# Rounded head means and a second half ordered by input tile, in the retention stage of a two-block transformer kernel

## The reference, cut to what matters

```python
def head_group_norm(y):
    yf = y.astype(jnp.float32)
    mu = jnp.mean(yf, axis=-1, keepdims=True)
    var = jnp.mean(jnp.square(yf - mu), axis=-1, keepdims=True)
    return (yf - mu) * lax.rsqrt(var + GN_EPS)
...
    ret = head_group_norm(ret).reshape(ret.shape[0], seq, RET_WIDTH)
    ret = (jax.nn.silu(rg.astype(jnp.float32)) * ret).astype(x.dtype)
    mixed = jnp.concatenate([fox.astype(x.dtype), ret], axis=-1)
    h = h + mixed @ w_out[i]
```

## Time and profile before

| | us |
|---|---|
| median of 3 runs | 2307.85 (2307.75 to 2309.3) |
| the profiled execution | 2308.38 |
| its span in the profile | 2306.6 |
| TensorE busy (matmuls) | 2280.4, 99% of the span |
| GpSimd, VectorE, ScalarE busy | 1182.7, 1102.6, 854.6 |

### The profile page before, as it was taken

One profiled execution on the slowest core, in us unless ns is written; L12 is line 12 of the kernel. 1 busy time (PEld: TensorE's weight loads), 2 busy tenths in 40 slices (PEclk: granted clock), 3 DMA queues, 4 the chain that ended last, 5 costly groups with the idle time before them and its releaser, 6 DMA issues.

```text
span 2306.6 us, 34053 instructions
## 1 busy us (share of the span) xinstructions
PE 2280.4 (99%) x11030; PEld 1814.7 (79%) x11030; DVE 1102.6 (48%) x1876; ACT 854.6 (37%) x1295; POOL 1182.7 (51%) x1554
## 2 busy tenths in 40 slices
PE   8999999999999999999999999999999999999997
PEld 6777877688888888877688888887877788888886
DVE  5468857534312314446755253354256755242444
ACT  4354454554322224323443222245233343232254
POOL 5446653345545445543356556566534256555563
PEclk9999999999999999999999999999999999999999
DMA  4221112133223232333222323223332223323222
GB/s 169 87 92 51 56 65 87 56 100 118 95 97 109 82 100 91 112 128 101 92 86 93 107 89 109 83 82 110 102 131 93 78 101 100 101 91 109 82 92 83
DMA packets 67367, 219.64 MB, mean 95 GB/s; under 512 B 8368, under 2 KB 8752, under 8 KB 67264
## 3 DMA queue, kind: packets, MB, share of 16 engines
q1 hardware_dynamic: 58400, 197.66, 25.7%
q10 hardware_dynamic: 8864, 20.62, 2.8%
HBM read 211.92 MB, written 2.13 MB: 93 GB/s over the span
## 4 chain that ended last, share of the span: by engine, by line
issue 42%; POOL 39%; PE 14%; DVE 2%; POOLq 1%; ACT 1%; DMA 1%; DVEq 0%; ACTq 0%; SPq 0%
POOL w_lo L2069 38%; PE acc L335 4%; PE acc L337 4%; PE acc L336 4%; POOLq L2116 1%; PE sc L524 1%; PE po_pt L651 0%; PE po_pt L481 0%; PE sc L651 0%; PE po_pt L460 0%; POOLq L2065 0%; DMA x<-in_x 0%; DMA raw<-in_w_ple_gate 0%; POOLq L2077 0%; DVE x_queries L1627 0%
## 5 line engine op out<-in xcount | busy, mean ns | idle before, releaser
L2069 POOL TENSOR_TENSOR w_lo<-raw,w_hi 128x256 fp32r<-128x256 f32 x1486 | 1134.5, 797 | 1056.5 <-ACT w_hi L854 1052.9
L335 PE MATMUL acc<-act_hi,w_hi 128*128 128x512 f32 x1696 | 673.0, 397 | 9.1 <-DVE act_lo L1387 8.1
L337 PE MATMUL acc<-act_hi,w_lo 128*128 128x512 f32 x1696 | 661.9, 390 | 0.0
L336 PE MATMUL acc<-act_lo,w_hi 128*128 128x512 f32 x1696 | 661.2, 390 | 0.0
L854 ACT CAST w_hi<-raw 128x1024 fp32r<-128x1024 f32 (+1 forms) x388 | 390.6, 1017 | 407.3 <-PE acc L337 224.5
L335 PE MATMUL acc<-y_hi,w_hi 128*128 128x512 f32 x1068 | 421.1, 394 | 0.0
L337 PE MATMUL acc<-y_hi,w_lo 128*128 128x512 f32 x1068 | 416.0, 390 | 0.0
L336 PE MATMUL acc<-y_lo,w_hi 128*128 128x512 f32 x1068 | 415.7, 389 | 0.0
L335 PEld LDWEIGHTS acc<-act_hi,w_hi 128*128 128x128 f32 x1696 | 319.1, 188 | 80.1 <-issue 9.8
L337 PEld LDWEIGHTS acc<-act_hi,w_lo 128*128 128x128 f32 x1696 | 318.9, 188 | 67.6
L336 PEld LDWEIGHTS acc<-act_lo,w_hi 128*128 128x128 f32 x1696 | 319.4, 188 | 65.7 <-issue 1.9
(11 more groups left out here) (316 smaller groups left out, 2097.9 us busy)
## 6 DMA issues: line engine op xcount, KB each, us to landing
raw<-in_w_ffn_wide SPq DMA_DIRECT2D x120, 512.0 KB, 3.3
raw<-in_w_in SPq DMA_DIRECT2D x102, 512.0 KB, 3.3
raw<-in_w_rest SPq DMA_DIRECT2D x72, 512.0 KB, 3.2
raw<-in_w_gate SPq DMA_DIRECT2D x24, 512.0 KB, 3.2
raw<-in_w_ple_gate SPq DMA_DIRECT2D x16, 512.0 KB, 3.2
raw<-in_w_branch SPq DMA_DIRECT2D x24, 256.0 KB, 2.6
raw<-in_w_ffn_narrow SPq DMA_DIRECT2D x16, 384.0 KB, 3.0
swap<-wab ACTq DMA_DIRECT2D x64, 64.0 KB, 2.0
```

Of the source, the lines that this page charges most:

```text
L335: nc.tensor.matmul(dst, w[0], src[0], start=start, stop=False)
L336: nc.tensor.matmul(dst, w[0], src[1], start=False, stop=False)
L337: return nc.tensor.matmul(dst, w[1], src[0], start=False, stop=stop)
L2069: last = nc.gpsimd.tensor_tensor(w_lo[:, slot, cut], raw[:, slot % 2, cut], w_hi[:, slot, cut], ALU.subtract)
```

## The change

Two things are changed in the retention stage, once in each layer.

First, the head means. Before, TensorE multiplies the fp32 squares by the fp32 constant, one product for each pair. Now VectorE splits each pair's squares into a rounded high part and the rest (a cast and a subtraction into tiles 4 to 7 of `y_hi` and `y_lo`, which are free until `split_here` writes the same tiles later), and TensorE makes two rounded products for each pair with a rounded copy of the constant, which ScalarE writes once near the start of the kernel. The product of the last pair is moved behind the first half of panel 1. VectorE's gate products of the four pairs come after all four splits.

Second, the order of the projection's second half (input tiles 4 to 7 of panels 0 to 3). Before, it goes panel by panel. Now it goes input tile by input tile, over the four panels each time, so that all four panels finish in the last round.

```diff
+    head_mean_r = sb("head_mean_r", [P, P], F32R)
...
+    def square_parts(p):
+        return y_hi[:, p + 4, :], y_lo[:, p + 4, :]
...
+                pe.wait_ge(S("mean_rounded"), 1)
                 for p in range(PAIRS):
-                    head_mean("r_sq", l * 4 + (p + 1), "r_var", p, square_r(p), ret_bank)
-                for j in range(1, 4):
+                    if p == PAIRS - 1:
+                        fox(1, range(4))
+                    pe.wait_ge(S("r_parts"), l * 4 + (p + 1))
+                    for half in range(2):
+                        last = nc.tensor.matmul(ret_bank[p], head_mean_r[:, :], square_parts(p)[half],
+                                                start=half == 0, stop=half == 1)
+                    last.then_inc(S("r_var"), 1)
+                for j in range(2, 4):
                     fox(j, range(4))
-                for j in range(4):
-                    for k in range(4, KD):
-                        if j == 0:
-                            pe.wait_ge(S("r_y"), l * 4 + (k - 3))
+                for k in range(4, KD):
+                    pe.wait_ge(S("r_y"), l * 4 + (k - 3))
+                    for j in range(4):
                         last = fox(j, (k,))
-                    last.then_inc(gemm_done, 1)
+                        if k == KD - 1:
+                            last.then_inc(gemm_done, 1)
...
             act.wait_ge(S("const_loaded"), 32)
+            nc.scalar.copy(head_mean_r[:, :], c["head_mean"]).then_inc(S("mean_rounded"), 1)
...
                 for p in range(PAIRS):
                     dve.wait_ge(S("r_sq"), l * 4 + (p + 1))
+                    high_part, low_part = square_parts(p)
+                    v.tensor_copy(high_part, square_r(p))
+                    dve.drain()
+                    v.tensor_tensor(low_part, square_r(p), high_part, ALU.subtract).then_inc(S("r_parts"), 1)
+                for p in range(PAIRS):
                     v.tensor_tensor(wb[:, p + 4, :], wb[:, p + 4, :], wa[:, p, :], ALU.mult)
```

## The result

The changed kernel takes 2316.2 us (median of 8 runs, 2313.22 to 2317.17); the kernel before took 2308.33 us beside it (8 runs, 2307.75 to 2309.3). The ratio is 1.0032, 95% interval 1.0023 to 1.004. So it is 7.9 us slower, where I had forecast 3.4, and above the upper end of my range. The profiled execution took 2317.17 us, its span is 2315.4, that of before 2306.6: 8.8 us more to find. Its mean granted TensorE clock is 0.996.

The account below looks back on a forecast made before the run. TensorE was taken to bound the kernel. Gain 3.2 us from the means and loss 6.5 to 6.6 from the late supply made 3.4 us net over 2307.85: 2311.2 us, range 2308.5 to 2315.5.

Parts of the forecast that it names:

- What bounds the kernel: Whole kernel: TensorE, matmuls busy 99% of the span, sets the time; microseconds gained or lost reach the end unless waits intervene.
- The rounded means: Head means: eight rounded products take 1.93 us instead of 3.54 for four fp32 ones, a gain of 1.6 us per layer.
- The splits and what is late behind them: VectorE at the head means: splits cost TensorE 0.1 us; later tiles up to 2.4 us late, none waited for.
- The supply: Panel 4's weights: low part ready 5.3 us after panel 0's last matmul, at 1174.2; TensorE waits 3.1 us per layer.
- that rival: After panel 4: supply stays behind for more than one panel, 1 to 2 us per layer, 2313 to 2315.5 us; 7%.
- The clock: Behind panel 4's wait: rival that TensorE's clock falls, 1.5 to 3 us per layer, 2314.3 to 2317.3 us; 13%.

Follow-up runs that it names:

- e1: The changed kernel with its rounded means, but the projection's second half panel by panel again: 2308.21 us, ratio 0.9999.
- e5: The changed kernel with 12 extra rounded products, result unread, filling TensorE's wait ahead of panel 4: 2312.05 us, ratio 1.0017.
- e3: The changed kernel with the second half reordered so that panel 0 finishes early, panels 0 and 1 sharing tiles: 2305.8 us, ratio 0.9987.
- e4: The changed kernel with tiles 4 and 5 over the four panels, then 6 and 7 panel by panel: 2308.09 us, ratio 0.9999.
- e2: The kernel before, with fp32 means, and only the second half taken tile by tile: 2319.7 us, ratio 1.0047.
- e7: The changed kernel run again, unedited, on the chip of the later experiments: 2315.95 us, ratio 1.0031.
- e8: The changed kernel with panel 0 finished early, plus 5 dummy products at the layer boundary and 6 in the last norm: 2306.45 us, ratio 0.999.

## Why the prediction was wrong

**What bounds the kernel** was right: each microsecond that TensorE lost in the stage reached the end.

**The rounded means** save 1.4 us in the first layer, not 1.6. Panel 4 could have started at 1171.27, 21.23 us behind the head means' start, against 22.62 before. The new products take 0.23 us each. The third pair is 0.09 us late (1150.86 to 1151.18, a step of 0.32), about the 0.1 that I charged for its split; what I left out is that the step behind this small wait costs 0.11 more once again (1151.18 to 1151.52). In the second layer the third pair isn't late, and the saving is the 1.6 of the forecast.

**The splits and what is late behind them** were otherwise right. The last tile's low part starts at 1162.38, done at 1163.07, forecast 1163.2, and no tile is waited for in the tile order. e1 shows that this cover is needed.

**The supply** was right in mechanism and size: panel 0's last matmul forecast 1168.9, measured 1168.99; panel 4 in effect at 1174.35 forecast (1174.24 and 0.11 for the restart), measured 1174.35 with the 0.11 still to come. e5 is this forecast without the clock: 3.6 us over before, where I had 3.4. e3 and e4 say the same from the other side, and e2 that the means have no part in it. The supply had caught up by panel 6, where the timeline has no further wait: that rival is out.

**The clock** is the step that failed: the sum has no term for matmuls at the lower level behind the wait, and the runs show 3.9 us for it in both layers together (e7 against e5). I gave the case that the wait brings the clock down 13%, and its price, 1.5 to 3 us per layer, holds what was measured: 1.6 and 1.6 us in the profile after, 1.6 and 2.9 in e7. In the sum I charged nothing for it. The reason I gave was the 1.80 us wait near the end of the kernel before, with matmuls only slightly slower behind it. That was a wrong reading in two ways. A wait of 1.80 us says nothing of one of 3.1. And it isn't a safe case itself: in the profiles of e2 and e4 the same wait is followed by two records at the full level, then a wait of 0.3 us, and then two at the lower one. In e4:

```profile
2296.32 2.07 PE L852 MATMUL sc<-probs,consts 128*128 128x512 f32 x2 [0.33 <-ACT probs L1318]
```

where the same two records take 1.12 us in the profile after. So the case was in the prediction with a fitting price, and with too small a chance. The trace had one other gap to judge by, the start, and there TensorE was at the lower level behind the idleness. The Trainium skill ("TensorE: Matmul & The Clock Gate", Why this matters for your kernels) warned of idle gaps between bursts. I put a gap of 3.1 us at the border of its rule. Measured, the clock fell behind all six gaps of 2.92 to 2.94 us and behind the one of 2.14, so here shorter gaps than that border count, and the measurement decides.

The traces show the clock's fall behind each wait of 2.92 to 2.94 us: two in the profile after, two in e7, two in e2. They show it behind the one wait of 2.14 us and, two records later, behind two of nine of 1.80 us, and not behind 0.92, 1.34 and 1.58 us. My forecast for the profiled execution was 2311.8; with the three pieces of the profile after it is 2311.8 + 1.6 + 1.6 + 1.8 = 2316.8, measured 2317.17. The boundary's share (1.8, wait and clock together) varies between executions, and the second layer's does too, so this sum is one execution's and not a law. What sets how many matmuls run at the lower level (7 to 9 in most cases, 14 in one) and how soon they begin (at once, or up to six matmuls later) stays open. So does whether the late load at the boundary comes from the change. Its one sighting is no evidence for that.

## What to carry to other kernels

Before matmuls are reordered so that several panels end together, look who gets the first panel's slot, and add up the chain from its last matmul to the first use by the successor (here 5.3 us); a new order has to leave that much work of other panels behind it. A wait of the matmul engine costs more than its length if its clock falls behind it: here 2.9 us of wait cost up to 2.9 more. Where the wait must stay, dummy matmuls in it gave back the clock's share (e5); look in the trace whether they stand where they were meant to (in e8 five did not). Where the order is free, finishing the panel whose slot is wanted first (e3) removes both.

## What the runs showed of the hardware that I had not expected

The clock does not fall during the wait alone. It can fall after matmuls have resumed at full speed: three at 0.23 us (first layer) or six (second layer) came first in the profile after, none in e7. So neither the length of the wait nor the first matmul behind it shows this loss; the granted clock by windows (0.66) and the distance between starts (0.43 instead of 0.23 us) do. And the changed kernel spreads more from run to run: 2313.2 to 2317.2 us against 2307.5 to 2309.6 for the kernel before, and 2311.6 to 2313.1 with the wait filled (e5). That this comes from such waits isn't shown: e2 has them too, and its five runs lie within 1 us.
